# A gated recurrence in four heads: scores made once per tile, masks in rounded passes, scalings on ScalarE, row turns moved into the stage before

## The reference, cut to what matters

```python
dmat = jnp.where(tri, b[..., :, None] - b[..., None, :] + ib[..., None, :], -jnp.inf)
inter = b + m[..., None]
m_t = jnp.maximum(inter, dmat.max(axis=-1))
w_intra = jnp.exp(dmat - m_t[..., None])
w_inter = jnp.exp(inter - m_t)
s = jnp.einsum("bhtd,bhsd->bhts", qb, kb) * w_intra
num = jnp.einsum("bhts,bhsv->bhtv", s, vb) + w_inter[..., None] * jnp.einsum("bhtd,bhdv->bhtv", qb, C)
den = s.sum(axis=-1) + w_inter * jnp.einsum("bhtd,bhd->bht", qb, n)
h = num / jnp.maximum(jnp.abs(den), jnp.exp(-m_t))[..., None]
C_new = decay[..., None, None] * C + jnp.einsum("bhs,bhsd,bhsv->bhdv", wk, kb, vb)
```

## Time and profile before

| | us |
|---|---|
| median of 3 runs | 3461.98 (3451.91 to 3465.14) |
| profiled execution, its time | 3469.53 |
| its span, first to last instruction | 3467.7 |
| mean granted clock of PE, as a share of 2.4 GHz | 0.962 |

### The profile page before, as it was taken

One profiled execution on the slowest core, in us unless ns is written; L12 is line 12 of the kernel. 1 busy time (PEld: TensorE's weight loads), 2 busy tenths in 40 slices (PEclk: granted clock), 3 DMA queues, 4 the chain that ended last, 5 costly groups with the idle time before them and its releaser, 6 DMA issues. The chain is left out here.

```text
span 3467.7 us, 47792 instructions
## 1 busy us (share of the span) xinstructions
PE 3178.4 (92%) x18624; PEld 2725.4 (79%) x18624; DVE 1784.8 (51%) x2658; ACT 1110.7 (32%) x1638; POOL 309.6 (9%) x268
## 2 busy tenths in 40 slices
PE   1999986999999799879999899999999899999997
PEld 1678775888888468758888897899999898778885
DVE  8548578544545647553333434554344334654353
ACT  2353233222222253233434333233223332243222
POOL 3000101011011100112222100010001100010001
PEclk9999888999999899889999999999999999999998
DMA  6201022222322402012222211122222211122322
GB/s 254 65 15 61 9 101 106 111 103 104 121 97 109 143 1 76 8 62 94 94 92 96 73 45 43 49 74 86 101 87 91 80 43 49 49 91 86 108 87 89
DMA packets 102581, 282.03 MB, mean 81 GB/s; under 512 B 35960, under 2 KB 36088, under 8 KB 100768
## 3 DMA queue, kind: packets, MB, share of 16 engines
q1 hardware_dynamic: 97568, 262.39, 21.6%
q0 software_dynamic: 4000, 11.98, 1.0%
q10 hardware_dynamic: 864, 5.57, 0.4%
HBM read 277.77 MB, written 2.10 MB: 81 GB/s over the span
## 5 line engine op out<-in xcount | busy, mean ns | idle before, releaser
L337 PE MATMUL ps<-h_hi,hi_ring 128*128 128x512 f32 (+1 forms) x2416 | 830.7, 344 | 74.6 <-DVE h_lo L641 41.7
L337 PE MATMUL ps<-h_lo,hi_ring 128*128 128x512 f32 (+1 forms) x2416 | 801.2, 332 | 0.0
L337 PE MATMUL ps<-h_hi,lo_ring 128*128 128x512 f32 (+1 forms) x2416 | 798.3, 330 | 0.0
L256 ACT ACTIVATE hi_ring<-ring 128x1024 fp32r<-128x1024 f32 (+1 forms) x410 | 419.9, 1025 | 1163.9 <-PE ps L337 1116.4
L266 DVE TENSOR_TENSOR lo_ring<-ring,hi_ring 128x1024 fp32r<-128x1024 f32 (+1 forms) x410 | 487.5, 1189 | 591.4 <-ACT hi_ring L256 587.2
L337 PEld LDWEIGHTS ps<-h_hi,hi_ring 128*128 128x128 f32 x2416 | 464.4, 192 | 151.2 <-issue 87.1
L337 PEld LDWEIGHTS ps<-h_lo,hi_ring 128*128 128x128 f32 x2416 | 465.8, 193 | 45.3 <-issue 3.3
L337 PEld LDWEIGHTS ps<-h_hi,lo_ring 128*128 128x128 f32 x2416 | 463.5, 192 | 42.3
L337 PE MATMUL ps<-ffn_operand,hi_ring 128*128 128x264 f32 (+1 forms) x2112 | 479.7, 322 | 1.5 <-DVE lo_ring L266 1.5
L337 PEld LDWEIGHTS ps<-ffn_operand,hi_ring 128*128 128x128 f32 x2112 | 350.2, 188 | 35.1 <-issue 1.8
L337 PE MATMUL ps<-ffn_operand,lo_ring 128*128 128x264 f32 (+1 forms) x1056 | 339.1, 321 | 0.0
(11 more groups left out here) (335 smaller groups left out, 3867.6 us busy)
## 6 DMA issues: line engine op xcount, KB each, us to landing
ring<-weights_dram SPq DMA_DIRECT2D x334, 512.0 KB, 3.2
mod_ring<-w_mod_dram SPq DMA_DIRECT2D x64, 512.0 KB, 4.3
ring<-weights_dram SPq DMA_DIRECT2D x76, 384.0 KB, 2.9
arena<-w_mod_dram SPq DMA_DIRECT2D x32, 512.0 KB, 3.5
x<-x_dram SPq DMA_DIRECT2D x1, 3072.0 KB, 16.9
arena<-c_rows_dram ACTq DMA_DIRECT2D x3, 1024.0 KB, 7.2
arena<-ret_decay_dram POOLq DMA_DIRECT2D x2, 1056.0 KB, 6.1
silu_rows<-c_rows_dram ACTq DMA_DIRECT2D x2, 1024.0 KB, 5.3
```

Source lines behind the costliest of these rows:

```text
L256: self.nc.scalar.activation(self.hi_ring[:, g % SPLIT, 0:w], self.ring[:, g % RING, 0:w], ACT.Copy).then_inc(self.hi, 1)
L337: ins = nc.tensor.matmul(out[0:m, c:c + n], w, a[:, t0:t0 + n], start=first and k == 0 and p == 0, stop=last and k == kts - 1 and p == 2)
```

## The change

All of it is in the two stages above, in both layers.

- The rows that are turned, the turned keys and the six small tables from them move into `mlstm_inputs`: `turn_keys` in n = 0 to 2, `turn_rows` behind the last weight block, their copies with them. For this ACT takes the four exponentials in n = 3, before the gates' next sigmoid, and not behind n = 5.
- The exponent product uses rounded operands (fp32r): the masks are rounded copies made by ACT at the stage's start, each head's row is held as a head and a rest (`top_parts`, rows 0 to 35 and 64 to 99), and a column of the identity, read 128 times, picks both. The `select` table and its load go.
- The scores are made in a tile's first unit only, scaled and copied to SBUF by ACT; DVE multiplies from there.
- ACT scales the state's part (`scale_part`) and divides (`divide`), four instructions each, one per head. DVE adds the two directions (`join`) and makes the moments there. All but two tiles are normalised before the last `join`.
- 16 passes of 512 columns, whose result nobody reads, run on PE before the first `weigh`.
- POOL's product of gain and gate moves from before its first keys to behind its second.

```diff
+TOP_LO = 64
+HOLD = 16
...
+        with nc.sbuf_tensor("top_parts", [P, ALL], F32R) as top_parts:
+            self.top_parts = top_parts
...
+            def turn_keys(n):
+
+                if n == 0:
+                    pe.wait_ge(made.sem, made.at(QK_BLOCKS))
+                for t in (2 * n, 2 * n + 1):
+                    if t >= 2:
+                        pe.wait_ge(keys_in.sem, keys_in.at(t - 1))
+                    for h in range(M_HEADS):
+                        last = nc.tensor.transpose(core.ps[:, 6 + t % 2, h * M_DIM:(h + 1) * M_DIM],
+                                                   m.k[0:M_DIM, h, t * P:(t + 1) * P], core.ident(M_DIM))
+                    last.then_inc(k_turned.sem, 1)
+
+            def turn_rows():
+
+                pe.wait_ge(keys_in.sem, keys_in.at(TT))
+                pe.wait_ge(rows_ready.sem, rows_ready.at(1))
+                for q, rows in enumerate((ai, m.w_state, m.floor, m.w_key)):
+                    for t in range(TT):
+                        n = q * TT + t
+                        nc.tensor.transpose(core.ps[:, 6 + n // 12, n % 12 * ROWS:(n % 12 + 1) * ROWS],
+                                            rows[:, t * P:(t + 1) * P], core.ident(ROWS))
+                pe.wait_ge(turned_in.sem, turned_in.at(turns - 1))
+                nc.tensor.matmul(core.ps[:, 5, 2 * P:2 * P + ROWS * TT], core.ones[0:ROWS, :],
+                                 m.decay_rows.rearrange("p r t -> p (r t)"), start=True,
+                                 stop=True).then_inc(rows_turned.sem, 1)
...
+                    if j - QK_BLOCKS - 2 < TT // 2:
+                        turn_keys(j - QK_BLOCKS - 2)
+            turn_rows()
...
-            act.wait_ge(exponents.sem, exponents.at(1))
-            for ap, sign in ((m.dec, 1.0), (m.w_state, 1.0), (m.floor, -1.0), (m.w_key, 1.0)):
-                step(nc.scalar.activation(ap, ap, ACT.Exp, scale=sign))
+                if n == 3:
+                    act.wait_ge(exponents.sem, exponents.at(1))
+                    for ap, sign in ((m.dec, 1.0), (m.w_state, 1.0), (m.floor, -1.0), (m.w_key, 1.0)):
+                        step(nc.scalar.activation(ap, ap, ACT.Exp, scale=sign))
+                    nc.scalar.activation(core.top_parts[0:ROWS, :], m.top, ACT.Copy).then_inc(top_hi.sem, 1)
...
+            def rows_out():
+                dve.wait_ge(act_chain.sem, act_chain.at(7))
+                v.tensor_scalar(m.w_state, m.w_state, float(M_DIM) ** -0.5, None, ALU.mult)
+                v.tensor_tensor(m.decay_rows, core.const[0:ROWS, C_IDENT:C_IDENT + ROWS][:, :, None].to_broadcast(
+                    [ROWS, ROWS, TT]), m.dec[:, None, :].to_broadcast([ROWS, ROWS, TT]),
+                    ALU.mult).then_inc(rows_ready.sem, 1)
+                dve.wait_ge(top_hi.sem, top_hi.at(1))
+                step(v.tensor_tensor(core.top_parts[TOP_LO:TOP_LO + ROWS, :], m.top, core.top_parts[0:ROWS, :],
+                                     ALU.subtract))
...
+                elif n == TT // 2 + 1:
+                    rows_out()
...
+                for t in (2 * n, 2 * n + 1):
+                    dve.wait_ge(k_turned.sem, k_turned.at(t + 1))
+                    nc.vector.tensor_copy(m.k_tok[:, t, :], core.ps[:, 6 + t % 2, 0:mw]).then_inc(keys_in.sem, 1)
+            dve.wait_ge(rows_turned.sem, rows_turned.at(1))
+            for d in range(2):
+                r = slice(ROW0[d], ROW0[d] + M_HEADS)
+                for n in range(2):
+                    v.tensor_copy(m.per_token[:, 12 * n:12 * (n + 1), d, :],
+                                  core.ps[:, 6 + n, 0:12 * ROWS].rearrange("p (n r) -> p n r", r=ROWS)[:, :, r])
+                last = v.tensor_copy(m.decay[:, d, :, :],
+                                     core.ps[:, 5, 2 * P:2 * P + ROWS * TT].rearrange("p (r t) -> p r t", t=TT)[:, r, :])
+            step(last)
...
-            pool.dma_start(select[0:ROWS, :, :], dram["select"]).then_inc(select_in.sem, 16)
-
-            nc.gpsimd.tensor_tensor(m.out_gate[:, 0:nt, :], m.out_gate[:, 0:nt, :], m.gain_row[:, None, :].to_broadcast(
-                [P, nt, hid]), ALU.mult).then_inc(gated.sem, 1)
-            pool.wait_ge(gated.sem, gated.at(1))
-            pool.wait_ge(token_rows.sem, token_rows.at(2))
...
+                if n == 1:
+                    nc.gpsimd.tensor_tensor(m.out_gate[:, 0:nt, :], m.out_gate[:, 0:nt, :],
+                                            m.gain_row[:, None, :].to_broadcast([P, nt, hid]),
+                                            ALU.mult).then_inc(gated.sem, 1)
...
+                mask = masks[:, 2 if d == 0 else 1, :]
+                rows = slice(0, TOP_LO + ROWS)
+                nc.tensor.matmul(core.ps[:, n % 2, :], masks[:, 0, :], mask[:, None, :].to_broadcast([P, M_HEADS, P]),
                                  start=True, stop=False)
                 for h in range(M_HEADS):
-                    last = nc.tensor.matmul(core.ps[:, n % 2, h * P:(h + 1) * P], select[0:ROWS, d * M_HEADS + h, :],
-                                            tile(m.top, t), start=False, stop=h == M_HEADS - 1)
+                    last = nc.tensor.matmul(core.ps[:, n % 2, h * P:(h + 1) * P],
+                                            pick[rows, d, h:h + 1].to_broadcast([TOP_LO + ROWS, P]),
+                                            tile(core.top_parts[rows, :], t), start=False, stop=h == M_HEADS - 1)
                 last.then_inc(weights_p.sem, 1)
-                if n >= 2:
-                    pe.wait_ge(scored.sem, scored.at(n - 1))
+                if u not in firsts:
+                    return
+                s = firsts.index(u)
+                if s >= 2:
+                    pe.wait_ge(scores_in.sem, scores_in.at(s - 1))
...
+                if n >= 2:
+                    pe.wait_ge(both_in.sem, both_in.at(n - 1))
...
+                    if n_carried(u):
+                        pe.wait_ge(part_in.sem, part_in.at(n_carried(u)))
...
+            pe.wait_ge(masks_in.sem, masks_in.at(1))
+            pe.wait_ge(picks_in.sem, picks_in.at(1))
+
+            for n in range(HOLD):
+                nc.tensor.matmul(core.ps[:, 7, :], masks[:, 0, :], masks[:, 1, None, :].to_broadcast([P, M_HEADS, P]),
+                                 start=True, stop=True)
...
+            nc.scalar.activation(masks[:], core.const[:, 0:3 * P].rearrange("p (r n) -> p r n", r=3),
+                                 ACT.Copy).then_inc(masks_in.sem, 1)
+
+            def exponents(u):
...
+                if u in firsts:
+                    s = firsts.index(u)
+                    act.wait_ge(scores_p.sem, scores_p.at(s + 1))
+                    nc.scalar.activation(qk_scores[:, s, :], core.ps[:, 2 + s % 2, :], ACT.Copy,
+                                         scale=scale).then_inc(scores_in.sem, 1)
+
+            def scale_part(u):
+                d, i, t = steps_all[u]
+                n, c = n_out(u), n_carried(u)
+                act.wait_ge(summed.sem, summed.at(n + 1))
+                if c >= 2:
+                    act.wait_ge(both_in.sem, both_in.at(n_out(carried[c - 2]) + 1))
+                for h in range(M_HEADS):
+                    last = nc.scalar.activation(part[:, c % 2, of_head(h)], core.ps[:, 6, of_head(h)], ACT.Copy,
+                                                scale=token(1, t, d, h))
+                last.then_inc(part_in.sem, 1)
+
+            def divide(u):
+                d, i, t = steps_all[u]
+                n = n_out(u)
+                act.wait_ge(inverted.sem, inverted.at(n + 1))
+                dst = out[:, t, :]
+                if u in seconds:
+                    s = seconds.index(u)
+                    dst = second[:, s % 2, :]
+                    if s >= 2:
+                        act.wait_ge(joined.sem, joined.at(s - 1))
+                for h in range(M_HEADS):
+                    c = h * (M_DIM + 1)
+                    last = nc.scalar.activation(dst[:, h * M_DIM:(h + 1) * M_DIM], both[:, n % 2, c:c + M_DIM], ACT.Copy,
+                                                scale=den[:, n % 2, h:h + 1])
+                last.then_inc(divided.sem, 1)
+
+            def roots(first, last):
+
+                for n in range(first, last):
+                    t = tiles_done[n]
+                    act.wait_ge(mean_sq.sem, mean_sq.at(n + 1))
+                    g = ms[:, t * M_HEADS:(t + 1) * M_HEADS]
+                    nc.scalar.activation(g, g, ACT.Sqrt, bias=core.eps[:, 0:1], scale=1.0 / M_DIM).then_inc(root.sem, 1)
+
+            exponents(outs[0])
+            for n, u in enumerate(outs):
+                if n + 1 < len(outs):
+                    exponents(outs[n + 1])
+                else:
+                    roots(0, early)
+                if u in carried:
+                    scale_part(u)
+                divide(u)
+            roots(early, nt)
...
+            def weigh_scores(u):
+                n, s = n_out(u), first_of[steps_all[u][2]]
```

(38 more changed lines are left out.)

189 lines of the change are left out of this document (75 added, 114 removed).

## The result

The changed kernel takes 3433.39 us (median of 6 runs, 3430.65 to 3438.69) against 3462.76 us (median of 6 runs, 3451.91 to 3466.42): ratio 0.9922, 95% interval 0.9905 to 0.9938, faster by 0.8%. Predicted were 3431 us. The profiled execution took 3430.9 us, span 3429.1 us.

The account below looks back on a forecast made before the run. PE was taken to bound the program, a chain of hand-overs the new recurrence. Gains 18.0 + 19.3 + 0.8 + 0.7 + 1.7 - 2.8 = 37.7 us, less 3.7 and 3, left 31.0: 3431 us, range 3414 to 3452.

Parts of the forecast that it names:

- Who ends last, and PE's part: Recurrence units: no engine alone ends last; ACT's chain takes 4.5 or 5.1 us, PE needs 3.2 to 4.2.
- ACT's part: Recurrence units: exponentials 1.14 us, each four-instruction scaling 1.05, twice per unit, and the scores' copy 0.6 in first units.
- Rival (b): Recurrence rounds: ACT's scalings are dearer, rounds take 6.0 and 5.4 us, 15 us of gain, 3447 us; chance 0.18.
- Layer 0, loop: Layer 0, first weigh to last reciprocal: falls from 77.8 to 59.8 us, gain 18.0.
- DVE's small steps: Chain of 18 rounds: small DVE steps, slower when POOL works beside them, take 3.7 us off the gain.
- Layer 1, loop: Layer 1's recurrence: falls from 67.0 to 47.7 us, gain 19.3, with 13.6 until the first inverse.
- 3 for the clock: Layer 1's four state updates: PE busy about half the time, so a fall of the clock costs 3 us.
- Tails: Behind each layer's last reciprocal: DVE's work falls from 11.6 to 10.8 us and from 9.0 to 8.3.
- The ways in: Stretch into each recurrence: layer 0 from 15.2 to 13.5 us, layer 1 from 13.1 to 15.9, a loss of 2.8.
- third sign of being wrong: Weight blocks of the inputs: the forecast is wrong if PE waits for `lo_ring` there.
- Rival (d): Both recurrences run at 1.2 GHz, passes failing to hold the clock: 3486 us, or near 3468; chance 0.08.
- The sum: Whole kernel: stage gains of 37.7 us, less 3.7 and 3, give 31.0 us, 3431 us on the median.

Follow-up runs that it names:

- e_scale_dve: Changed kernel with the two scalings (carried part, division) made by DVE in one instruction each instead of by ACT in four: 3430.2 us, ratio to before 0.9909.
- e_hold0: Changed kernel with the 16 unread passes left out of both layers: 3424.4 us, ratio to before 0.9892.
- e_l1_order: Changed kernel, layer 1 alone reordered: DVE hands on two states before weighing first scores, PE's second weighing follows the first growth: 3427.8 us, ratio to before 0.9914.
- e_tail_passes: Changed kernel without the 16 passes, with 7 unread passes (4 in layer 1) at the end of the inputs' stage: 3427.2 us, ratio to before 0.9909.
- e_gate_split: e_tail_passes with GpSimd's product of output gates and gain cut into one instruction per tile: 3422.7 us, ratio to before 0.9895.
- e_fp32_weigh: Changed kernel with mask and row selection back in fp32, passes included: 3439.0 us, ratio to before 0.9932.
- e_best: Changed kernel with ACT and layer 1 reordered, passes moved to the inputs' tail, gates' product cut by tiles, last roots behind scaling: 3405.5 us, ratio to before 0.9840.

## Why the prediction was right, point by point

- **Who ends last, and PE's part.** Right. Mask 0.32 us (0.2), picks 0.39 (0.5), PE's unit about 3.2 and 4.2 us at 2.4 GHz, gaps at PEclk 1.00. That the loop of hand-overs sets the rounds was shown by the order of ACT (R -9.6 us with the same instructions) and by the fp32 version (PE's extra 1.36 us hidden but for 0.56).
- **ACT's part.** 1.05 for a scaling of 97 columns was right, 1.17 for the division of 96 (1.05), 0.6 for the copy. Rival (b), dearer scalings, took 0.12 of the 0.9 us that it needed. The Trainium skill's formula (ScalarE: Activation LUTs, What ACT_TABLE_LOAD costs, and not the rules section that the prediction names for it) gives by estimate about 1.2 us for four, near the division and above the scaling. The advice of the Trainium skill (ScalarE: Activation LUTs, Rules for kernel authors) to leave products to DVE is borne out only for the order of after: e_scale_dve shortened R by 4.9 us, the other order on ACT by 9.6.
- **Layer 0, loop.** 59.3 us (59.8; its parts as written add up to 59.7, and the start-up's named prices to 9.2 of its 10.5, with the second ACT round unpriced; measured is 10.5). Rounds 4.94 with a copy (5.1), 4.7 and 4.8 (4.5 and 4.85), last 5.6 (5.5). The clock's dip from 415.1 to 421.9 cost 0.35 us in two of them (4.73 and 4.71, where e_hold0 has 4.63 and 4.46 without the dip).
- **DVE's small steps, 3.7 us.** Mis-sized: of the 60 small steps of both layers three take more than 0.2 us (0.72, 0.42 and 0.45), 1.0 us too much in all. Where GpSimd's long instruction was the real danger, at the start, the passes stood over it. This term should have been near 1 and the next one larger.
- **Layer 1, loop.** The step that failed: 53.4 us, where 47.7 and 3 for the clock were told. The 3 us had the right place and too small a size. 13.6 us to the first inverse became 19.7, mainly since `pass_on` of the first state is queued behind `weigh_scores` on DVE, which waits for ACT's new copy. The prediction named the queue behind `part_in` and `divided`, not this one. e_l1_order removed the wait and the fall of the clock together: 8.5 us.
- **Tails.** 10.9 and 8.3 us (10.8 and 8.3).
- **The ways in.** The prediction counts the key turns' 1.3 us in. They took 1.4 in each layer, and PE's wait for `lo_ring` in layer 0 fell from 0.98 to 0.31, as told (the third sign of being wrong, a wait for `lo_ring`, is there by the letter, but it is the rest of an old wait):

```profile
330.76 0.50 PE L341 MATMUL ps<-h_hi,hi_ring 128*128 128x512 f32 x1 [0.31 <-DVE lo_ring L270]
```

  With them layer 0 has 15.0 us (13.5), since the passes took 6.6 (5), and layer 1 16.4 (15.9, of which 7.9 isn't itemised), with a wait of 1.70 for ACT (3) and 5.8 for the passes (5). The sentence from the Trainium skill (TensorE: Matmul & The Clock Gate, Part 4), that transposes don't count as busy for the clock, is in line with the trace of layer 0, which doesn't show it alone: the clock fell at 374.1, behind PE's turns (until 371.5) and 2.6 us of idle time, and the passes ran at 0.50 until 380.9. In e_tail_passes seven passes stood directly behind the same turns, and the clock stayed at 1.00. Whether turns alone would have let it fall, without idle time, no run here shows.
- **Rival (d), the clock.** It did not come, but it rested on a wrong reading, that the passes are what keeps the clock. Without any pass the new units had it at 1.00 again after 10.2 us in layer 0 and 20.4 in layer 1 (e_hold0). Its sign, PEclk 0.50 for more than 10 us in a recurrence, did come, for 13.6 us in layer 1. With the 2.07 us wait that stood before it, it cost at most about the 8.5 us that e_l1_order took away, not the 17 us and more that would have made this rival.
- **The sum.** The changed stages gained 30.5 us, with the key turns counted in, where 31.0 were told, and the medians 29.4. That they are so near is in part luck, since misses cancel: -2.7 us in layer 1's loop beyond its 3, -1.5 and -0.5 on the ways in, against +3.7 for the small steps, which the measured loops already contain, and +0.5 in layer 0's loop.
- **What it did not ask.** The range priced what the parts might cost, but not whether a part was worth its price: three of them (the passes, the scores made once with their copy on ACT, and the order given to ACT) each cost 9 to 11 us by the medians against a version without it. They share layer 1's start, so their costs don't add. Nor does any single part explain the gain: of the 31.6 us in the stretches, the rounding taken back alone gives up 3.9, and the scores made twice, the scalings on DVE and no passes give up nothing. Scores made twice in fp32, which would give PE its old unit of 5.5 us, was not run, nor were the moved turns taken back.

## What to carry to other kernels

When a bound engine gets shorter units, the next limit is often a loop of hand-overs and not an engine: write down each engine's order, and look for work of a later unit that could stand where an engine waits. Each pass that only lifts the clock must be held against doing the real work at half clock for that long. Work that moves to another stage is to be measured there too, from that stage's own start and not by the time on the clock of the whole run. Ahead of a copy that is shared between units, look at what is queued behind its reader at the start, where nothing hides it.

## What the runs showed of the hardware

- The recurrence's own units brought the granted clock back from 0.50 to 1.00 without any pass (375.9 to 386.1 and 1372.6 to 1393.0 in e_hold0; with 16 passes 374.1 to 380.9 and 1374.2 to 1384.5 in the changed kernel). A fall followed on PE's wait of 2.07 us in layer 1 of all four kernels that have it, and on one of 2.79 us in e_tail_passes (at 383.5).
- GpSimd's 128x2304 product held DVE's products of 128x512 that read and wrote SBUF: 4.08 us for two instead of 1.38, the first ending 0.55 us behind GpSimd's end (e_tail_passes). Beside GpSimd's products of 128x384 DVE's steps of 4 columns took 0.72 and 0.92 us instead of 0.17 (e_gate_split).
- At a granted clock of 1.00, four rounded products of 128 columns on 100 rows take 0.39 us, 0.10 each, and what follows the rounded mask of 512 columns starts 0.32 us behind it; in fp32 they take 0.27 each and 0.98 (e_fp32_weigh).
- The granted clock differs between executions of one kernel: the four runs of e_best spread over 10 us, the slowest with a mean of 0.963 and the others with 0.966 to 0.968. The slowest is the profiled one, with 27 us at 0.50 in layer 1.
